# VectorE instead of GpSimd adds the squares of the three inner pre-norms

## The reference, cut to what matters

```python
def rms_norm(x, g):
    y = xf * lax.rsqrt(jnp.mean(xf * xf, axis=-1, keepdims=True) + RMS_EPS) * g
for layer in range(DEPTH):                      # DEPTH = 2
    h = rms_norm(x, norm_mix_pre[layer])
    m = even_mixer(h, ...) if layer % 2 == 0 else odd_mixer(h, ...)
    x = x + rms_norm(m, norm_mix_post[layer])
    h = rms_norm(x, norm_ffn_pre[layer])
    f = conv_ffn(h, ...)                        # up 1024 -> 2*2816, conv, gelu gate, down
    x = x + rms_norm(f, norm_ffn_post[layer])
```

## Time and profile before

| what | us |
|---|---|
| median of three runs | 1075.27 |
| profiled execution, its own time | 1075.82 |
| its span (first to last instruction) | 1074.0 |
| TensorE busy | 1064.7 |
| VectorE busy | 683.4 |
| ScalarE busy | 478.0 |
| GpSimd busy | 58.8 |

### The profile page before, as it was taken

How to read it: one execution, slowest core, us unless ns; L and a number is a source line. 1 busy time by engine, 2 the same in 40 slices (tenths; PEclk the granted TensorE clock), 3 DMA queues, 4 the chain that set the end, 5 groups by cost and what they waited for, 6 DMA issues and landing times.

```text
span 1074.0 us, 14619 instructions
## 1 busy us (share of the span) xinstructions
PE 1064.7 (99%) x5782; PEld 899.0 (84%) x5782; DVE 683.4 (64%) x890; ACT 478.0 (45%) x694; POOL 58.8 (5%) x55
## 2 busy tenths in 40 slices
PE   9999999999999999999999999999999999999997
PEld 7876889988888888888899877998888888888886
DVE  6685875977767676522247777398776767663323
ACT  6454764644344343412236366465434434341321
POOL 0000002300000000001103000131000000000000
PEclk9999999999999999999999999999999999999999
DMA  7342141123222222222332623212323223234542
GB/s 239 118 118 70 49 143 63 70 79 110 87 97 99 85 110 82 105 97 80 109 117 63 178 72 119 97 61 79 113 84 101 95 84 111 84 112 92 144 118 79
DMA packets 39847, 107.71 MB, mean 100 GB/s; under 512 B 20721, under 2 KB 23537, under 8 KB 29169
## 3 DMA queue, kind: packets, MB, share of 16 engines
q1 hardware_dynamic: 39648, 106.94, 30.2%
q10 hardware_dynamic: 144, 0.01, 0.0%
HBM read 98.15 MB, written 2.10 MB: 93 GB/s over the span
## 4 chain that ended last, share of the span: by engine, by line
PE 96%; ACT 1%; DMA 1%; SPq 1%; issue 1%; DVE 0%; DVEq 0%; ACTq 0%
PE ps L1662 31%; PE ps L1664 30%; PE ps L1663 30%; PE ps L1827 1%; PE ps L1853 1%; PE ps L1838 1%; PE ps L2113 1%; PE ps L2102 1%; DMA w_raw<-in_odd_w_o 1%; PE ps L2129 1%; ACT prob L1093 0%; DMA w_raw<-in_even_w_in 0%; SPq L565 0%; PE ps L1735 0%; PE ps L1719 0%
## 5 line engine op out<-in xcount | busy, mean ns | idle before, releaser
L1662 PE MATMUL ps<-hx_hi,w_hi 128*128 128x512 f32 x812 | 320.3, 394 | 0.2 <-DVE w_lo L1163 0.2
L1664 PE MATMUL ps<-hx_hi,w_lo 128*128 128x512 f32 x812 | 316.5, 390 | 0.0
L1663 PE MATMUL ps<-hx_lo,w_hi 128*128 128x512 f32 x812 | 316.3, 390 | 0.0
L1140 DVE TENSOR_TENSOR w_lo<-w_raw,w_hi 128x2048 fp32r<-128x2048 f32 (+1 forms) x74 | 167.7, 2266 | 115.5 <-ACT w_hi L731 115.4
L731 ACT ACTIVATE w_hi<-w_raw 128x2048 fp32r<-128x2048 f32 (+1 forms) x76 | 142.1, 1871 | 127.0 <-DMA w_raw<-in_ffn_w_down 112.4
L1662 PEld LDWEIGHTS ps<-hx_hi,w_hi 128*128 128x128 f32 x812 | 152.5, 188 | 35.8 <-issue 4.6
L1664 PEld LDWEIGHTS ps<-hx_hi,w_lo 128*128 128x128 f32 x812 | 152.5, 188 | 32.0
L1663 PEld LDWEIGHTS ps<-hx_lo,w_hi 128*128 128x128 f32 x812 | 152.6, 188 | 30.8 <-issue 0.5
L1007 ACT ACTIVATE cg<-ug,vec 128x512 f32<-128x512 f32 x44 | 35.9, 816 | 136.5 <-DVE ug L1474 136.5
L1483 DVE SCALAR_TENSOR_TENSOR cg<-ug,vec,cg 128x511 f32<-128x511 f32 x88 | 65.8, 748 | 20.4 <-ACT cg L1007 20.4
L1019 ACT ACTIVATE g_hi<-cv 128x512 f32 (+1 forms) x44 | 27.8, 632 | 111.1 <-DVE cv L1492 111.1
(11 more groups left out here) (252 smaller groups left out, 1851.8 us busy)
## 6 DMA issues: line engine op xcount, KB each, us to landing
w_raw<-in_ffn_w_up SPq DMA_DIRECT2D x40, 1024.0 KB, 4.8
w_raw<-in_ffn_w_down SPq DMA_DIRECT2D x16, 1024.0 KB, 5.0
w_raw<-in_even_w_in SPq DMA_DIRECT2D x6, 1024.0 KB, 4.8
w_raw<-in_even_w_out SPq DMA_DIRECT2D x3, 1024.0 KB, 4.8
w_raw_s<-in_odd_w_qkv SPq DMA_DIRECT2D x3, 1024.0 KB, 4.8
w_raw<-in_odd_w_qkv SPq DMA_DIRECT2D x3, 1024.0 KB, 5.6
w_raw<-in_odd_w_o SPq DMA_DIRECT2D x3, 1024.0 KB, 5.0
rsw<-rp SPq DMA_DIRECT2D x40, 64.0 KB, 2.0
```

What stands on the lines that cost most here:

```text
L1140: dve.tensor_tensor(w_lo[s][:, 0:k], w_raw[s][:, 0:k], w_hi[s][:, 0:k], ALU.subtract).then_inc(w_lo_done, 1)
L1662: pe.matmul(dst, s_hi, r_hi, start=first, stop=False)
L1663: pe.matmul(dst, s_hi, r_lo, start=False, stop=False)
L1664: return pe.matmul(dst, s_lo, r_hi, start=False, stop=last)
```

## The change

The seven adds of each inner pre-norm leave GpSimd's program and go to VectorE's, as `pre_sum`, a form of `first_sum` that takes the number of the norm. In half B, add i - 1 stands behind the rest, norm and add of tile i, from i = 2 on; the seventh stands behind the loop, ahead of `split_lo(splits[2])`. ScalarE's and TensorE's programs are the same, and so are the semaphores and their counts.

```diff
     @block.gpsimd
-        def pre_norm(p):
-            for i in range(1, DT):
-                pool.wait_ge(sq_done, DT * p + i + 1)
-                ...
-                    ins = pool.tensor_tensor(sumsq[:], sumsq[:], sq[i % 2][:], ALU.add)
-                ins.then_inc(sum_done, 1)
...
         last_sum(0, 1)
-        pre_norm(1)
...
     @block.vector
-        def first_sum(i):
-            dve.wait_ge(sq_done, i + 1)
+        def pre_sum(p, i):
+            dve.wait_ge(sq_done, DT * p + i + 1)
             if i == 1:
+                if p:
+                    dve.wait_ge(pms_mm, 2 * p)
                 ins = dve.tensor_tensor(sumsq[:], sq[0][:], sq[1][:], ALU.add)
             else:
-                dve.wait_ge(sum_done, i - 1)
+                dve.wait_ge(sum_done, pre_sums(p) + i - 1)
                 ins = dve.tensor_tensor(sumsq[:], sumsq[:], sq[i % 2][:], ALU.add)
             ins.then_inc(sum_done, 1)
...
                     if i + 2 < DT:
                         normed(h, i + 2)
                         add(h, i + 2)
+                    if h and i >= 2:
+                        pre_sum(bi + 1, i - 1)
                 if h == 0:
                     if bi != 1:
                         split_lo(splits[0])
                     split_lo(splits[1])
+            pre_sum(bi + 1, DT - 1)
             split_lo(splits[2])
             dve.wait_ge(rbc_done, bi + 2)
```

More of the change, by code:

```diff
@@ L713, in _ @@
         last_sum(1, 1)
-        pre_norm(2)
         whole_sums(2, 2)
@@ L718, in _ @@
         last_sum(2, 1)
-        pre_norm(3)
     @block.scalar
@@ L1195, in _ @@
             if i >= 3:
-                first_sum(i - 2)
+                pre_sum(0, i - 2)
         for i in (DT - 2, DT - 1):
-            first_sum(i)
+            pre_sum(0, i)
         dve.wait_ge(const_in, 16)
```

## The result

| | before | changed |
|---|---|---|
| first measurement, median of 4 (us) | 1075.23 (1074.9 to 1076.15) | 1082.29 (1079.8 to 1084.48) |
| profiled execution: own time, span (us) | 1075.82, 1074.0 | 1079.8, 1077.6 |
| its mean granted clock | 0.999 | 1.000 |

The ratio is 1.006, 95% interval 1.0048 to 1.0073: slower. The profiled execution is 4.0 us slower than that of before (span 3.6), where 3.3 was forecast; the 0.4 between the two is time outside the span, 2.2 us here and 1.82 before. But it is the fastest of the four. The other three took 1082.16, 1082.41 and 1084.48 us, with mean clocks of 0.996, 0.996 and 0.997. So there are two things to explain: the waits, and something more that comes in some executions.

The account below looks back on a forecast made before the run. The prediction took TensorE, busy 99% of the span, to bound the kernel. New waits of 1.4 us at boundary 2 and 1.9 at boundary 1 gave +3.3 on 1075.27, so 1078.6 us, range 1075.4 to 1080.4.

Parts of the forecast that it names:

- What bounds the kernel: TensorE, busy 99% of the span; time moves only with its waits; slack 0.1 us at boundary 1, nothing at boundary 2.
- What goes and what comes: VectorE in half B: 4.6 us back per boundary without GpSimd's adds, 4.4 us of new adds, an even exchange.
- What the order adds: VectorE idles for ScalarE: 1.2 us ahead of rest 3, 1.1 ahead of rest 6, or 0.86 ahead of boundary 1's rest 4.
- The sum of the waits: TensorE's lateness: +1.4 us at boundary 2, +1.9 at boundary 1, nothing at boundary 0, together +3.3 us.
- The rest of the program ... I take 0: After boundary 1 all engines stay about 1.9 us later, with nothing caught up in the attention stretch: 0.
- More than forecast: Rival: waits at boundary 0 too and 0.80 us per add, 1080.8 us; chance 0.06.
- The removal of GpSimd's instructions by itself is worth 0: Taking the adds out of GpSimd's program changes the time by 0, since GpSimd waits most of the time.
- The even trade: Rival: VectorE gets back what it gives, no idle times, TensorE loses its 0.47 us wait at boundary 2: 1074.8; chance 0.13.
- Only one of the two stalls: Rival: boundary 1's wait partly caught up or boundary 2's rest 6 in time, +1.4 to +1.9 us; chance 0.12.

Follow-up runs that it names:

- three_split_first: The changed kernel with three buffers of squares instead of two and the seventh add behind the last weight split; median 1075.88 us, ratio 1.0002.
- again: The changed kernel measured once more, with no edit, on another chip; median 1079.36 us, ratio 1.0042.
- delay_b1: The kernel before with one useless VectorE instruction over three tiles ahead of boundary 1's last weight split; median 1076.2 us, ratio 1.0003.
- split_first: The changed kernel with the seventh add behind the boundary's last weight split instead of ahead of it; median 1079.47 us, ratio 1.0037.
- three_buffers: The changed kernel with the squares of the inner pre-norms in three buffers instead of two; median 1076.1 us, ratio 1.0003.
- b02_only: The changed kernel with adds of squares on VectorE only at boundaries 0 and 2, on GpSimd at boundary 1; median 1077.48 us, ratio 1.0018.
- b1_only: The changed kernel with adds of squares on VectorE only at boundary 1, on GpSimd at boundaries 0 and 2; median 1079.27 us, ratio 1.003.

## Why the prediction was wrong

The forecast was 1078.6, the range 1075.4 to 1080.4; the median was 1082.29. By its own steps:

- **What bounds the kernel**: right in where the waits came, at the slacks of 0.1 and 0 us. "So the time moves only where TensorE starts to wait or stops waiting" is not: in the executions with a fall it moved, too, where TensorE was busy all the time at half speed.
- **What goes and what comes**: right. Rests at 0.48, the split at 2.28, adds at 0.68. By work alone the exchange is even: three_split_first keeps all 21 adds on VectorE at 1.0002.
- **What the order adds**: right and shown. 1.10 us of idle time ahead of rest 3 (said 1.2), 1.05 ahead of rest 6 (said 1.1), 0.79 ahead of rest 4 at boundary 1 (said 0.86). With a third buffer, the 1.4 us of boundary 2 turn into -0.46.
- **The sum of the waits**: right. 1.96 and 1.41 against 1.9 and 1.4, and no wait of TensorE at boundary 0. Boundary 1's k = 6 waited 0.2 us inside the larger wait, as allowed for.
- **"The rest of the program ... I take 0"**: this is the step that failed. It looked only for a gain, bounded by "nothing regained". Behind boundary 1 there was a further loss: the granted clock went to its lower level behind the wait of 1.9 us. All seven long executions of the changed kernel, of 15, have a lower mean clock on record (0.995 to 0.997). In the two profiles that caught the fall in kernels with the change it lasted 6.8 us and cost 2.2 to 3.0 us from u2 to n2. In the first measurement three of four executions were of this kind, so the median held it: 1079.8 + 2.5. That share was bad luck: over all 15 executions it is 7, and their median is 1080.4. No rival had TensorE's clock in it, and "More than forecast" reached 1080.8 by way of dearer adds, which did not happen.
- **"The removal of GpSimd's instructions by itself is worth 0"**: off by some 0.35 us, a smaller miss. An execution's own time is longer than its span by 2.0 to 2.3 us in all 47 executions of the kernels in which GpSimd makes none of the inner adds, and by 1.7 to 1.9 in all others. The span does not show where this time goes; the cause is open.
- **The even trade**: refuted as the outcome (two idle times of 1.1 us), though its sum of work was right. **Only one of the two stalls**: refuted, each stall passed in full to the end (343.83 from e to the end in both kernels; 129.95 from u2 to n2 in again, 129.93 before).

The chance of slower (0.74) was on the right side. Executions without the fall took 1079.0 to 1080.4 us, 0.4 to 1.8 above the forecast, which is the other part of the miss: the 0.35 us outside the span, and scatter that I had not allowed for (u2 to n2 took 130.47 in the first profile and 129.95 in the next, and 129.93 before).

The Trainium skill's page "TensorE: Matmul & The Clock Gate" (Part 1: The HAM clock gate) says that an idle TensorE falls to 1.2 GHz and goes back to 2.4 GHz only after sustained work. The traces agree on the two levels (0.50 and 1.00 in the windows above) and on the delayed return: TensorE was busy all the time for 3.4 and 6.8 us before the clock rose. The fall itself came 0.03 to 1.0 us after TensorE had started again. Read ahead of the forecast, the page would have made a fall of the clock behind the new wait a rival of its own.

What stays open: the executions of 1084.48 and 1085.52 are some 5 us above the short ones, twice what the profiled falls cost. A longer stretch at the lower level, or a second one, would lower the mean clock further. The 1085.52 has 0.995, the lowest of its kernel, but the 1084.48 has 0.997, no lower than the executions of 1081.4 to 1082.4 (0.996), so a longer fall does not account for it; no profile caught either. Nor is it shown that only the new wait does this: of the kernel before the four longest of 26 executions on one chip (1076.9 to 1077.9, median 1075.6) all have a mean clock of 0.998, and none was profiled.

## What to carry to other kernels

Before an operation moves to a busier engine, follow the semaphores that its result releases: if the instruction right behind it, on the same engine, hangs on them through another engine's queue, each such place costs a round trip (here 1.1 us), however even the exchange of work is. Here one more buffer took the loss away (1.0003 of before instead of 1.0042 and more), with the adds on the same engine.

Where TensorE is the bound, price a new wait of it twice, as the wait and as the chance that the clock falls behind it; a median of few executions then lies in either group. If the wait can't be removed, matmuls that nobody reads can stand in its place: here no fall came in five executions with them.

## What the runs showed of the hardware

- Behind waits of 1.88 us at boundary 1 the clock fell in some executions and not in others of the same kernel; a wait of 3.76 us was followed by a fall even in the fastest of its five executions; waits of 1.06 to 1.37 us at boundary 1 and of 1.3 us at boundary 2 were followed by none in a profile, and in delay_b1, split_first, three_buffers and b02_only every execution has a mean clock of 0.998 or more.
- A GpSimd add holds up VectorE instructions with two SBUF operands (1.55 us instead of 0.48) and not those with a PSUM operand (0.48), and the exchange is so even that VectorE, with 21 instructions more, was busy 682.0 us instead of 683.4.
- Matmuls of 256 columns go at two paces with the granted clock at 1.00. In half B of boundary 1 they start 0.1178 us apart in before and in b1_only, and 0.1135 in the changed kernel, three_buffers and most others; at boundary 0 it is 0.1176 to 0.1178 in all, at boundary 2 0.1131 to 0.1136 in all. Over 96 matmuls that is 0.4 us, so the slack of 0.1 us read from one execution at boundary 1 was the largest, not the usual one: in b02_only, whose boundary 1 is that of before, TensorE waits 0.54 us for the split. What decides the pace is open.
